# Gate and up products of a column block back to back, and one Block for both halves of the channel mixer

## The chip, the cores and the metric

The kernel runs on one core of a Trainium2 chip. The metric is the device time in microseconds (us) of one execution. Before the change it is 3491.59 us, the median of three runs (3485.54 to 3496.79). A core has five engines, each with its own instruction stream: TensorE (PE in the profile, with its weight loads as PEld), VectorE (DVE), ScalarE (ACT), GpSimd (POOL) and SyncE (SP), which here issues most DMAs. Engines meet only through semaphores.

## The reference, cut to what matters

One decoder layer is computed for 2048 prompt tokens and 8 sample tokens. The change is in its last part, the channel mixer (`conv_ffn`), with the residual sum and the final RMSNorm behind it:

```python
gate, up = jnp.split(h @ w_up, 2, axis=-1)            # D_MODEL 1024 -> 2 x D_FF 2816
g = causal_dwconv(jnp.concatenate([buf, gate], 1), conv_w, conv_b)   # 3 taps along the tokens
f = (jax.nn.silu(g) * up) @ w_down                    # 2816 -> 1024
y = rmsnorm(x2 + f, final_norm_w)
```

The last two gate rows of each group and the sample tokens' gates are outputs too.

## The kernel before, in words

`channel_mixer` (L1848) is called twice by `program`, once for a half of the tokens. Half 1 has 8 tiles of 128 prompt tokens and the 8 sample tokens (9 token tiles, three blocks of 344 columns in a product); half 2 has 8 tiles (two blocks of 512). Each call opens a Block of its own: tensors are placed anew, all engines meet at its end, and nothing of the second call starts before.

Inside, a trip (11 in each half, L1928) works off two column blocks `s` = 0, 1 of D_FF, 128 columns each. Every product is made from a high and a low part of both operands, as three matmuls (hi·hi, hi·lo, lo·hi). In a trip the engines do this, each in the order of its own stream:

- PE: gate products of s=0 into `g_ps`, gate of s=1 into `g_ps`, up of s=0 into `u_ps`, up of s=1 into `u_ps` (`project_up`, L2150 to L2162); then for each token tile n the down product, two 512-column sums of 6 matmuls each (L2182 to L2184), into `y_ps` for even n and into `g_ps` for odd n (`sums`). Tile n waits until the add of tile n-2 has emptied its sum (`added`), and a new trip waits for all adds of the one before (`pe.wait_ge(added, i * YT + 2)`).
- ACT: the high part of the up weights of both s (`up_hi`, L2020), each as soon as PE has done the last product with that buffer; for each s the copies of the gate sums to SBUF (L2026) and the silus (L2030); the high part of both down weights (`dn_hi`, L2035). With the loop closed, `up_hi` of the next trip follows `dn_hi` of this one.
- POOL: `up_lo` = raw - hi of s=0 and of s=1 (L1998, 128x2048), then `dn_lo` of both (L2003, 128x1024), each after its ACT part.
- DVE: `convolve` of s=0 and of s=1 (L2080, L2085), then `multiply` of s=0 and of s=1: for each block gate times up sum (L2113), a CAST to `a_hi` (L2114) and the difference `a_lo` (L2115); then the adds of all token tiles into `y` (L2126). The adds stand behind all of `multiply` in DVE's stream.
- SP: loads, each when its buffer is free.

At a half's start the h tiles are loaded and split into hi and lo (L2011, L2055), and after all of them the first up weights. At its end ACT squares each tile (L2039), one root serves all tiles (L2042), DVE scales them (L2137) and ACT stores them (L2046).

Of the kernel before, what the change touches and what calls it, by code (L numbers as in the profile page):

```python
# [1846 lines left out]
def channel_mixer(nc, tag, sample, first_tile, h2_d, x2_d, w_up_d, w_down_d, small_d, final_w_d,  # L1847
                  edge, y_p_d, y_s_d, s_gate_d):  # L1848
# [4 lines left out]
    TT = TILES // 2  # L1853
    NT = TT * P + (DEC if sample else 0)
    widths = [344] * 3 if sample else [512] * 2
    nb = len(widths)
    at = [sum(widths[:b]) for b in range(nb + 1)]
    assert at[nb] == NT
    YT = TT + (1 if sample else 0)
    NA = YT * P  # L1860
    W = widths[0]
    HALO = FFN_CONV - 1
    TRIPS = FF_TILES // 2
    with ExitStack() as ctx:
# [24 lines left out]
        sq = sb("sq", [P, YT])  # L1889
# [3 lines left out]
        g_ps = ps("g", [P, nb, 512])  # L1893
        u_ps = ps("u", [P, nb, 512])
# [16 lines left out]
        a_hi_ready, a_ready = sem("a_hi_ready"), sem("a_ready")  # L1911
# [15 lines left out]
        def over_trips(eng, body, steps=None, per=0):
            with eng.Fori(0, TRIPS) as i:  # L1928
                if steps:
                    with steps.loop(i, TRIPS, per):  # L1930
                        body(i)
                else:
                    body(i)

        @block.sync
        def _(sp):
            def weights_up(i, s):
                sp.dma_start(up_raw[:, s], w_up_d[bass.ds(i * 2 + s, 1)].rearrange("a p k n -> (a p) k n")
                             ).then_inc(up_landed[s], 16)
# [12 lines left out]
            for n in range(2, len(tiles)):

                sp.wait_ge(h_landed[n % 2], 16 * (n // 2))
                load_h(n)
            for n in range(len(tiles)):
                sp.wait_ge(h_ready, n + 1)
                load_x2(n)

            def body(i):  # L1960
                for s in range(2):

                    sp.wait_ge(conv_ready, (i * 2 + s + 1) * nb)
                    sp.dma_start(small[:, s], small_d[bass.ds(i * 2 + s, 1)].rearrange("a p n -> (a p) n")
                                 ).then_inc(small_landed[s], 16)
                for s in range(2):

                    sp.wait_ge(dn_ready, i * 2 + s + 1)
                    sp.dma_start(dn_raw[:, s], w_down_d[bass.ds((i * 2 + s) * P, P), :]).then_inc(dn_landed[s], 16)

            def ahead(i):
                for s in range(2):

                    sp.wait_ge(up_ready, i * 2 + s + 3)
                    weights_up(i + 1, s)

            with sp.Fori(0, TRIPS - 1) as i:
                body(i)
                ahead(i)
            body(TRIPS - 1)  # L1980

            sp.wait_ge(dn_ready, FF_TILES + 1)
            sp.dma_start(dn_raw[:, 0], final_w_d.rearrange("(a n) -> a n", a=1).broadcast_to([P, D_MODEL])
                         ).then_inc(y_landed, 16)

        @block.gpsimd
        def _(pool):
            pool.memset(a_hi[:, :, NT:].bitcast(F32), 0.0) if sample else None
            pool.memset(a_lo[:, :, NT:].bitcast(F32), 0.0).then_inc(setup, 1) if sample else pool.sem_inc(setup, 1)
# [3 lines left out]
            def body(i):  # L1993
                for s in range(2):

                    pool.wait_ge(up_hi_ready, i * 2 + s + 1)
                    pool.wait_ge(upped, (i * 2 + s + 1) * nb)
                    pool.tensor_tensor(up_lo[:, s], up_raw[:, s], up_hi[:, s].bitcast(F32), ALU.subtract  # L1998
                                       ).then_inc(up_ready, 1)
                for s in range(2):  # L2000
                    pool.wait_ge(dn_hi_ready, i * 2 + s + 1)
                    pool.wait_ge(downed, i * YT + 1)
                    pool.tensor_tensor(dn_lo[:, s], dn_raw[:, s], dn_hi[:, s].bitcast(F32), ALU.subtract  # L2003
                                       ).then_inc(dn_ready, 1)
            over_trips(pool, body)

        @block.scalar
        def _(act):
            for n, (t, c, w) in enumerate(tiles):
                act.wait_ge(h_landed[n % 2], 16 * (n // 2 + 1))  # L2010
                act.activation(h_hi[:, :, c:c + w], stage[:, n, :, 0:w], ACT.Copy).then_inc(h_hi_ready, 1)  # L2011

            act.sem_inc(gate_ready, nb)
            act.sem_inc(act_ready, 1)

            def body(i):
                for s in range(2):
                    act.wait_ge(up_landed[s], i * 16 + 16)
                    act.wait_ge(upped, (i * 2 + s + 1) * nb)
                    act.activation(up_hi[:, s], up_raw[:, s], ACT.Copy).then_inc(up_hi_ready, 1)  # L2020
                for s in range(2):
                    n0 = (i * 2 + s) * nb
                    for b in range(nb):
                        act.wait_ge(gated, n0 + b + 1)
                        act.wait_ge(prod_ready, n0 + nb)
                        act.activation(gate[:, s, HALO + at[b]:HALO + at[b + 1]], g_ps[:, b, 0:widths[b]], ACT.Copy  # L2026
                                       ).then_inc(gate_ready, 1)
                    for b in range(nb):
                        act.wait_ge(conv_ready, n0 + 2 * nb + b + 1)
                        act.activation(gate[:, s, at[b]:at[b + 1]], conv[:, 0:widths[b]], ACT.Silu  # L2030
                                       ).then_inc(act_ready, 1)
                for s in range(2):
                    act.wait_ge(dn_landed[s], i * 16 + 16)
                    act.wait_ge(downed, i * YT + 1)
                    act.activation(dn_hi[:, s], dn_raw[:, s], ACT.Copy).then_inc(dn_hi_ready, 1)  # L2035
            over_trips(act, body)
            for n in range(YT):
                act.wait_ge(added, (TRIPS - 1) * YT + n + 3)
                act.activation(gate[:, 0, 0:D_MODEL], y[:, n], ACT.Square, accum_out=sq[:, n:n + 1]).then_inc(squared, 1)  # L2039
                act.wait_ge(squared, n + 1)  # L2040
            act.wait_ge(mean_ready, 1)
            act.activation(root[:], sq[:], ACT.Sqrt).then_inc(rooted, 1)  # L2042
            for n, (t, c, w) in enumerate(tiles):
                act.wait_ge(y_done, n + 1)
                dst = y_s_d if t == 0 else y_p_d[(t - 1) * P:t * P, :]
                act.dma_start(dst, y[0:w, n]).then_inc(stored, 16)  # L2046
            if sample:
                act.dma_start(s_gate_d, s_gate[:]).then_inc(stored, 16)
            act.wait_ge(stored, 16 * (YT + (1 if sample else 0)))

        @block.vector
        def _(v):
            for n, (t, c, w) in enumerate(tiles):
                v.wait_ge(h_hi_ready, n + 1)
                v.tensor_tensor(h_lo[:, :, c:c + w], stage[:, n, :, 0:w], h_hi[:, :, c:c + w].bitcast(F32),  # L2055
                                ALU.subtract).then_inc(h_ready, 1)
            if sample:
                v.memset(edge[:], 0.0).then_inc(setup, 1)
            else:
                v.sem_inc(setup, 1)  # L2060
            v.wait_ge(setup, 2)
            v.sem_inc(prod_ready, 2 * nb)
            v.sem_inc(conv_ready, 2 * nb)
# [933 lines left out]
```

## Time and profile before

| | us |
|---|---|
| median of the runs | 3491.59 |
| the profiled execution's own time | 3495.07 |
| its span, first to last instruction | 3492.8 |
| PE matmul busy in it | 3033.5 (87%) |
| DVE, ACT, POOL busy | 1599.7, 884.7, 756.5 |

The channel mixer takes the last 1645 us: its first load is issued at 1847.9, half 1's matmuls run from 1880.9 to 2678.2, half 2's from 2728.9 to 3472.3, and the span ends at 3492.8. The granted clock of PE is 1.00 (2.4 GHz) in a steady trip and 0.50 (1.2 GHz) after long pauses. A matmul's record is longer than its step, because matmuls overlap; times of work on PE are best read as the distance from one start to another.

### The profile page before, as it was taken

To read this page: it belongs to the slowest core of one execution; us is meant where nothing else is said; L and a number is where in the kernel's file an instruction comes from. 1 tells how busy PE (TensorE), PEld (TensorE's weight loads), DVE (VectorE), ACT (ScalarE), POOL (GpSimd) and SP (SyncE) were. 2 spreads that over 40 slices of the span, in tenths; PEclk is the share of its full clock that TensorE was granted. 3 is DMA by queue.
4 is the path that set the end of the run, shared out by engine and by line. 5 is a ranking of instruction groups with operands and counts; after the bars stand their busy time and mean duration, and the time that the engine had idled before them with its cause. 6 is when DMAs were issued, how large, how long until landed. Compare 5 with 4: busy or idle time off the path is not lost. (4 is left out here: it accounts for less than half of the span.)

```text
span 3492.8 us, 45919 instructions
## 1 busy us (share of the span) xinstructions
PE 3033.5 (87%) x16539; PEld 2602.2 (75%) x16539; DVE 1599.7 (46%) x2940; ACT 884.7 (25%) x1649; POOL 756.5 (22%) x547
## 2 busy tenths in 40 slices
PE   8999999699997998107894999999996799999997
PEld 6888889576675998006774988998886678878876
DVE  5113111366775888342333544454445434444444
ACT  4123222233332555002223111221112212112212
POOL 4002000244441555002111211122110212211220
PEclk9999999889998999558997999999998899999998
DMA  4454324657752333353435111111102411111101
GB/s 148 177 192 167 112 92 147 166 169 203 201 179 74 85 96 81 105 116 127 144 126 199 48 48 36 36 48 53 44 12 92 157 36 47 60 38 36 60 24 54
DMA packets 227714, 352.66 MB, mean 101 GB/s; under 512 B 73518, under 2 KB 161191, under 8 KB 221592
## 3 DMA queue, kind: packets, MB, share of 16 engines
q1 hardware_dynamic: 219281, 302.07, 28.4%
q10 hardware_dynamic: 7360, 26.34, 1.9%
q0 software_dynamic: 944, 22.61, 1.7%
q8 instruction: 71, 1.16, 0.1%
q14 instruction: 58, 0.48, 0.0%
HBM read 286.16 MB, written 93.95 MB: 109 GB/s over the span
## 5 line engine op out<-in xcount | busy, mean ns | idle before, releaser
L2159 PE MATMUL cm_g_ps<-cm_h_hi,cm_up_hi 128*128 128x344 f32 (+1 forms) x880 | 309.7, 352 | 120.4 <-POOL cm_up_lo L1998 88.3
L2826 PE MATMUL pj_acc<-pj_w_hi,pj_h_hi 128*128 128x480 f32 (+5 forms) x952 | 357.1, 375 | 8.3 <-DVE pj_w_lo L2726 8.3
L2827 PE MATMUL pj_acc<-pj_w_lo,pj_h_hi 128*128 128x480 f32 (+5 forms) x952 | 355.9, 374 | 0.0
L2828 PE MATMUL pj_acc<-pj_w_hi,pj_h_lo 128*128 128x480 f32 (+5 forms) x952 | 355.6, 374 | 0.0
L2003 POOL TENSOR_TENSOR cm_dn_lo<-cm_dn_raw,cm_dn_hi 128x1024 fp32r<-128x1024 f32 x44 | 107.8, 2469 | 995.4 <-ACT cm_dn_hi L2035 995.4
L2161 PE MATMUL cm_g_ps<-cm_h_hi,cm_up_lo 128*128 128x344 f32 (+1 forms) x880 | 307.4, 349 | 0.0
L2160 PE MATMUL cm_g_ps<-cm_h_lo,cm_up_hi 128*128 128x344 f32 (+1 forms) x880 | 307.3, 349 | 0.0
L2159 PE MATMUL cm_u_ps<-cm_h_hi,cm_up_hi 128*128 128x344 f32 (+1 forms) x880 | 306.9, 349 | 0.0
L2161 PE MATMUL cm_u_ps<-cm_h_hi,cm_up_lo 128*128 128x344 f32 (+1 forms) x880 | 305.6, 347 | 0.0
L2160 PE MATMUL cm_u_ps<-cm_h_lo,cm_up_hi 128*128 128x344 f32 (+1 forms) x880 | 305.6, 347 | 0.0
L2159 PEld LDWEIGHTS cm_g_ps<-cm_h_hi,cm_up_hi 128*128 128x128 f32 x880 | 166.6, 189 | 142.8 <-issue 129.2
L1998 POOL TENSOR_TENSOR cm_up_lo<-cm_up_raw,cm_up_hi 128x2048 fp32r<-128x2048 f32 x44 | 204.2, 4642 | 282.9 <-ACT cm_up_hi L2020 282.9
L2026 ACT ACTIVATE cm_gate<-cm_g_ps 128x344 f32<-128x344 f32 (+1 forms) x110 | 55.3, 513 | 799.1 <-PE cm_g_ps L2161 798.2
L2726 DVE TENSOR_TENSOR pj_w_lo<-pj_w_raw,pj_w_hi 128x480 fp32r<-128x480 f32 (+3 forms) x112 | 76.4, 703 | 393.9 <-ACT pj_w_hi L2681 393.9
L2080 DVE TENSOR_SCALAR cm_conv<-cm_gate,cm_small 128x344 f32<-128x344 f32 (+2 forms) x110 | 54.3, 494 | 374.0 <-ACT cm_gate L2030 223.4
L2826 PEld LDWEIGHTS pj_acc<-pj_w_hi,pj_h_hi 128*128 128x128 f32 (+1 forms) x952 | 175.5, 184 | 34.3 <-issue 8.6
L371 POOL TENSOR_TENSOR fp_prod<-fp_kv,fp_q_own 128x1024 f32<-128x1024 f32 x64 | 151.6, 2369 | 226.8 <-DVE fp_s_dec L414 226.8
L2828 PEld LDWEIGHTS pj_acc<-pj_w_hi,pj_h_lo 128*128 128x128 f32 (+1 forms) x952 | 174.9, 184 | 25.9 <-issue 1.3
L2827 PEld LDWEIGHTS pj_acc<-pj_w_lo,pj_h_hi 128*128 128x128 f32 (+1 forms) x952 | 175.0, 184 | 25.1 <-issue 1.0
L2126 DVE TENSOR_TENSOR cm_y<-cm_y,cm_y_ps 128x1024 f32<-128x1024 f32 x99 | 120.9, 1221 | 144.9 <-PE cm_y_ps L2184 144.9
L2659 ACT ACTIVATE pj_row<-pj_acc,pj_rstd 128x480 f32<-128x480 f32 (+6 forms) x119 | 76.2, 641 | 409.0 <-PE pj_acc L2828 373.7
L2159 PEld LDWEIGHTS cm_u_ps<-cm_h_hi,cm_up_hi 128*128 128x128 f32 x880 | 165.2, 188 | 16.0 <-DVE cm_a_lo L2115 2.7
(429 smaller groups left out, 6658.2 us busy)
## 6 DMA issues: line engine op xcount, KB each, us to landing
fp_kv<-in_fox_kv SPq DMA_DIRECT2D x256, 256.0 KB, 3.0
cm_up_raw<-in_w_up SPq DMA_DIRECT2D x44, 1024.0 KB, 4.8
cm_dn_raw<-in_w_down SPq DMA_DIRECT2D x44, 512.0 KB, 3.5
out_s_win<-in_cache POOLq DMA_DIRECT2D x8, 2047.0 KB, 9.6
proj_a<-pj_row SPq DMA_DIRECT2D x48, 240.0 KB
sp_raw<-proj_b SPq DMA_DIRECT2D x16, 640.0 KB, 4.0
pj_w_raw<-in_w_a SPq DMA_DIRECT2D x10, 960.0 KB, 8.1
dp_raw<-proj_a SPq DMA_DIRECT2D x48, 192.0 KB, 3.4
```

The costliest lines, as they stand in the source:

```text
L371: pool.tensor_tensor(prod[:, n % 2], kv[:, at:at + QUART, 0], q_own[:, a // 2:a // 2 + 1].to_broadcast([P, QUART, F]), ALU.mult).then_inc( ...
L1998: pool.tensor_tensor(up_lo[:, s], up_raw[:, s], up_hi[:, s].bitcast(F32), ALU.subtract).then_inc(up_ready, 1)
L2003: pool.tensor_tensor(dn_lo[:, s], dn_raw[:, s], dn_hi[:, s].bitcast(F32), ALU.subtract).then_inc(dn_ready, 1)
L2126: v.tensor_tensor(y[:, n], y[:, n], sums(n).rearrange("p a n -> p (a n)"), ALU.add).then_inc(added, 1)
L2159: pe.matmul(out, hi, h_hi[:, k, cs], start=(k == 0), stop=False)
L2160: pe.matmul(out, hi, h_lo[:, k, cs], start=False, stop=False)
L2161: last = pe.matmul(out, lo, h_hi[:, k, cs], start=False, stop=(k == KT - 1))
L2659: act.activation(row[0:m, n % ROWS, 0:wide], acc[0:m, n % BANKS, 0:wide], ACT.Copy, scale=rstd[0:m, t:t + 1]).then_inc(evac, 1)
L2726: v.tensor_tensor(w_lo[:, j % 2, k, 0:n], w_raw[:, k, 0:n], w_hi[:, j % 2, k, 0:n].bitcast(F32), ALU.subtract).then_inc(w_ready, 1)
L2826: pe.matmul(out, h_hi[:, k, place(t)], w_hi[:, j % 2, k, 0:wide], start=(k == 0), stop=False)
L2827: pe.matmul(out, h_hi[:, k, place(t)], w_lo[:, j % 2, k, 0:wide], start=False, stop=False)
L2828: last = pe.matmul(out, h_lo[:, k, place(t)], w_hi[:, j % 2, k, 0:wide], start=False, stop=(k == KT - 1))
```

## The change

There is one call and one Block; a class `Half` holds the counts of each half, and all tensors keep the sizes of half 1. Four things differ:

1. PE's order in a trip is now gate s=0, up s=0, gate s=1, up s=1, and DVE's is convolve and multiply of s=0, then of s=1. The orders inside ACT's and POOL's trips are the same as before; ACT splits the next trip's up weights at the end of a trip, where it did so at the next one's start.
2. `sums` is counted from the end, so that the last token tile always sums into `y_ps`, and a trip begins when all but the last add are done.
3. The second half's h tiles go through the two `dn_raw` buffers and are split while half 1's last down products run; DVE puts each `finish_h` behind an add. Half 1's squares, root and scaling, and its stores (now on SP, three in flight), run beside half 2's first trip. At the very start the first up weights are split right after the first h tile.
4. The final norm of half 2 is cut into three parts (tiles 0 to 3, 4 and 5, 6 and 7), put between the last adds.

```diff
+        def sums(H, n):
+
+            return y_ps[:] if (H.yt - 1 - n) % 2 == 0 else g_ps[:, 0:2]
...
+            def load_h(m):
...
+                if m in (YT, YT + 1):
+
+                    sp.wait_ge(dn_ready, FF_TILES + m - YT + 1)
+                elif m > YT:
+                    sp.wait_ge(h_ready, m - 1)
+                sp.dma_start(h_raw(m), h2_d[H.tiles[m - H.tile0][0]]).then_inc(h_landed[k], 16)
...
+            split_h(0)
+            split_up(first, 0)
+            for m in range(1, YT):
+                split_h(m)
+            with act.Fori(0, TRIPS - 1) as i:
+                gates(first, i)
+                split_down(first, i)
+                split_up(first, i + 1)
+            gates(first, TRIPS - 1)
+            split_down(first, TRIPS - 1)
+            split_up(second, 0)
+            for m in range(YT, YT + second.yt):
+                split_h(m)
+            squares(first)
...
-            def body(i):
-                convolve(i, 0)
-                convolve(i, 1)
-                multiply(i, 0)
-                multiply(i, 1)
...
+            def middle(H, i):
+                for s in range(2):
+                    convolve(H, i, s)
+                    multiply(H, i, s)
...
+            middle(first, TRIPS - 1)
             for n in range(YT):
...
+                add(first, TRIPS - 1, n)
+                if n > 0:
+                    finish_h(YT + n - 1)
+            v.wait_ge(final_landed, 16)
+            scale_of(first, 0)
+            for n in range(YT):
+                normed(n)
+
+            trip(second, 0)
...
-            def body(i):
-                pe.wait_ge(added, i * YT + 2)
...
+            def trip(H, i):
+                nb, at = H.nb, H.at
+                pe.wait_ge(added, H.down0 + i * H.yt + 1)
                 for s in range(2):
-                    pe.wait_ge(up_ready, i * 2 + s + 3)
-                    project_up(i, s, 0, g_ps, gated)
-                for s in range(2):
-                    project_up(i, s, 1, u_ps, upped)
...
+                    pe.wait_ge(up_ready, H.ff0 + i * 2 + s + 3)
+                    project_up(H, i, s, 0, g_ps, gated)
+                    project_up(H, i, s, 1, u_ps, upped)
...
+                    pe.wait_ge(added, H.down0 + i * H.yt + max(n + 1, 2))
```

PE in half 2's trip, where the gate products of s=0 end (`cm_g_ps` holds gate sums, `cm_u_ps` up sums). Before:

```order
L2159 MATMUL cm_g_ps<-cm_h_hi,cm_up_hi 128x512
L2160 MATMUL cm_g_ps<-cm_h_lo,cm_up_hi 128x512
L2161 MATMUL cm_g_ps<-cm_h_hi,cm_up_lo 128x512
L2167 REGISTER_ALU
L2150 ISA
L2159 MATMUL cm_g_ps<-cm_h_hi,cm_up_hi 128x512
```

And of the change:

```order
L2313 MATMUL cm_g_ps<-cm_h_hi,cm_up_hi 128x512
L2314 MATMUL cm_g_ps<-cm_h_lo,cm_up_hi 128x512
L2315 MATMUL cm_g_ps<-cm_h_hi,cm_up_lo 128x512
L2308 REGISTER_ALU
L2313 MATMUL cm_u_ps<-cm_h_hi,cm_up_hi 128x512
L2314 MATMUL cm_u_ps<-cm_h_lo,cm_up_hi 128x512
```

What came next was the gate of s=1; now it is the up product of s=0, and the gate of s=1 stands a whole product phase later.

DVE in half 2's trip, behind the last `multiply` of s=0. Before:

```order
L2115 TENSOR_TENSOR cm_a_lo<-cm_gate,cm_a_hi 128x512
L2108 REGISTER_ALU
L2113 TENSOR_TENSOR cm_gate<-cm_gate,cm_u_ps 128x512
L75 REGISTER_ALU
L2114 CAST cm_a_hi<-cm_gate 128x512
```

And of the change (the first trip of half 2, which stands unrolled):

```order
L2218 TENSOR_TENSOR cm_a_lo<-cm_gate,cm_a_hi 128x512
L2176 COPY cm_gate<-edge 128x2
L2182 TENSOR_SCALAR cm_conv<-cm_gate,cm_small 128x512
L2187 SCALAR_TENSOR_TENSOR cm_conv<-cm_gate,cm_small,cm_conv 128x512 x2
L2182 TENSOR_SCALAR cm_conv<-cm_gate,cm_small 128x512
```

The convolution of s=1 moved behind the products of s=0; in both, `multiply` of s=1 and then the adds come last.

## Rows read from the trace of the kernel before

**Rows 1.** Waits of the channel mixer: who <- whom, us in total, times, longest.
```profile
PE cm_g_ps L2159 <- POOL cm_up_lo L1998: 88.3, 2, 50.8
PE cm_g_ps L2159 <- DVE cm_y L2126: 32.1, 20, 1.6
```
**Rows 2.** Stretches: length; busy (count) PE, PEld, DVE, ACT, POOL; PEclk, DMA share, GB/s.
```profile
2534.83:2607.30 72.47, 70.86 (x397) 65.59 (x397) 35.77 (x57) 13.67 (x18) 14.24 (x4) 1.00 0.05 15
2534.83:2557.57 22.74, 22.74 (x144) 22.74 (x145) 7.13 (x18) 4.83 (x9) 0.00 (x0) 1.00 0.01 0
...
3136.57:3204.07 67.50, 65.89 (x288) 53.91 (x289) 28.89 (x36) 13.12 (x14) 14.18 (x4) 1.00 0.14 47
3136.57:3158.46 21.89, 21.89 (x97) 18.10 (x97) 6.27 (x11) 4.35 (x6) 0.00 (x0) 1.00 0.00 0
...
3180.33:3202.40 22.07, 22.07 (x97) 17.84 (x95) 10.36 (x10) 1.92 (x1) 4.65 (x1) 1.00 0.14 50
```
**Rows 3.** Order of time, half 2: start, us, engine, instruction, [idle before <-releaser].
```profile
3162.57 1.99 ACT L2035 ACTIVATE cm_dn_hi<-cm_dn_raw 128x1024 fp32r<-128x1024 f32 x2
...
3169.54 1.92 ACT L2020 ACTIVATE cm_up_hi<-cm_up_raw 128x2048 fp32r<-128x2048 f32 x1 [3.67 <-PE cm_u_ps L2161]
...
3163.78 4.93 POOL L2003 TENSOR_TENSOR cm_dn_lo<-cm_dn_raw,cm_dn_hi 128x1024 fp32r<-128x1024 f32 x2 [44.02 <-ACT cm_dn_hi L2035]
...
3182.61 4.65 POOL L1998 TENSOR_TENSOR cm_up_lo<-cm_up_raw,cm_up_hi 128x2048 fp32r<-128x2048 f32 x1 [6.40 <-ACT cm_up_hi L2020]
...
3164.91 1.55 DVE L2114 CAST cm_a_hi<-cm_gate 128x512 fp32r<-128x512 f32 x1
3166.50 2.76 DVE L2115 TENSOR_TENSOR cm_a_lo<-cm_gate,cm_a_hi 128x512 fp32r<-128x512 f32 x1
...
3181.25 0.43 DVE L2114 CAST cm_a_hi<-cm_gate 128x512 fp32r<-128x512 f32 x1
3181.71 0.69 DVE L2115 TENSOR_TENSOR cm_a_lo<-cm_gate,cm_a_hi 128x512 fp32r<-128x512 f32 x1
3183.28 1.22 DVE L2126 TENSOR_TENSOR cm_y<-cm_y,cm_y_ps 128x1024 f32<-128x1024 f32 x1 [0.87 <-PE cm_y_ps L2184]
```
**Rows 4.** The same view, half 1.
```profile
2564.89 4.86 POOL L2003 TENSOR_TENSOR cm_dn_lo<-cm_dn_raw,cm_dn_hi 128x1024 fp32r<-128x1024 f32 x2 [50.21 <-ACT cm_dn_hi L2035]
2571.18 4.75 POOL L1998 TENSOR_TENSOR cm_up_lo<-cm_up_raw,cm_up_hi 128x2048 fp32r<-128x2048 f32 x1 [1.44 <-ACT cm_up_hi L2020]
...
2573.43 2.70 DVE L2114 CAST cm_a_hi<-cm_gate 128x344 fp32r<-128x344 f32 x1
```
**Rows 5.** The same view: PE's first matmuls after three pauses.
```profile
22.08 0.58 PE L2810 MATMUL pj_sum<-pj_ones,pj_sq 128*128 128x1 f32 x2 [5.62 <-POOL pj_sq L2642]
...
321.91 0.58 PE L2810 MATMUL pj_sum<-pj_ones,pj_sq 128*128 128x1 f32 x2 [6.18 <-POOL pj_sq L2642]
...
682.17 1.01 PE L805 MATMUL fp_z<-fp_consts,fp_m_tok 128*4 128x128 f32 x4 [5.89 <-DVE fp_m_tok L626]
```
**Rows 6.** Stretches right after the last two of them, columns as in rows 2.
```profile
321.90:328.10 6.20, 6.19 (x18) 5.82 (x19) 4.90 (x12) 3.21 (x5) 4.21 (x3) 0.50 0.38 120
...
682.20:686.50 4.30, 4.30 (x16) 3.56 (x17) 0.99 (x2) 0.59 (x1) 0.00 (x0) 0.50 0.79 252
```
**Rows 7.** Order of time at the two starts and the end.
```profile
1876.19 9.01 POOL L1998 TENSOR_TENSOR cm_up_lo<-cm_up_raw,cm_up_hi 128x2048 fp32r<-128x2048 f32 x2 [27.77 <-ACT cm_up_hi L2020]
...
2710.28 2.46 DVE L2055 TENSOR_TENSOR cm_h_lo<-cm_y,cm_h_hi 128x1024 fp32r<-128x1024 f32 x2 [5.18 <-ACT cm_h_hi L2011]
...
2720.82 1.23 DVE L2055 TENSOR_TENSOR cm_h_lo<-cm_y,cm_h_hi 128x1024 fp32r<-128x1024 f32 x1 [1.38 <-ACT cm_h_hi L2011]
...
2729.90 0.63 PE L2161 MATMUL cm_g_ps<-cm_h_hi,cm_up_lo 128*128 128x512 f32 x1
2730.33 0.63 PE L2159 MATMUL cm_g_ps<-cm_h_hi,cm_up_hi 128*128 128x512 f32 x1
...
3477.91 9.66 DVE L2137 SCALAR_TENSOR_TENSOR cm_y<-cm_y,cm_rstd,cm_dn_raw 128x1024 f32<-128x1024 f32 x8
```

More of the change, by code:

```diff
@@ L1971, in ahead, with load_small @@
[L1971 to L1975, printed above, removed]
-            with sp.Fori(0, TRIPS - 1) as i:
[L1978 to L1984, printed above, removed]
+            def load_small(H, i, s):
+                if not (H is first and isinstance(i, int) and i == 0):
+                    sp.wait_ge(conv_ready, H.two0 + (i * 2 + s + 1) * H.nb)
+                sp.dma_start(small[:, s], small_d[bass.ds(i * 2 + s, 1)].rearrange("a p n -> (a p) n")
+                             ).then_inc(small_landed[s], 16)
@@ L2041, in _, with squares @@
[L2041 to L2049, printed above, removed]
+            def squares(H):
+                for a, b in norms[halves.index(H)]:
+                    for n in range(a, b):
+                        act.wait_ge(added, H.down0 + (TRIPS - 1) * H.yt + n + 3)
+                        act.wait_ge(squared, H.tile0 + n)
+                        act.activation(gate[:, 0, HALO:HALO + D_MODEL], y[:, n], ACT.Square,
+                                       accum_out=sq[:, halves.index(H), n:n + 1]).then_inc(squared, 1)
+                    if H is second:
+                        act.wait_ge(mean_ready, 2 + norms[1].index((a, b)))
+                    else:
+                        act.wait_ge(mean_ready, 1)
+                    act.activation(root[:, a:b], sq[:, halves.index(H), a:b], ACT.Sqrt).then_inc(rooted, 1)
@@ L2057, in _, with finish_h @@
[L2057 to L2063, printed above, removed]
[L2064 to L2066 removed]
+            def finish_h(m):
+                H = first if m < YT else second
+                _, c, w = H.tiles[m - H.tile0]
+                v.wait_ge(h_hi_ready, m + 1)
+                v.tensor_tensor(h_lo[:, :, c:c + w], h_raw(m)[:, :, 0:w], h_hi[:, :, c:c + w].bitcast(F32),
+                                ALU.subtract).then_inc(h_ready, 1)
@@ new lines, in normed, with trip @@
+            def normed(n):
+                v.scalar_tensor_tensor(out=y[:, n], in0=y[:, n], scalar=rstd[:, n:n + 1], in1=final_w[:],
+                                       op0=ALU.mult, op1=ALU.mult).then_inc(y_done, 1)
+            def trip(H, i):
+                middle(H, i)
+                for n in range(H.yt):
+                    add(H, i, n)
+            for m in range(YT):
+                finish_h(m)
+            v.memset(edge[:], 0.0).then_inc(setup, 1)
+            v.wait_ge(setup, 2)
@@ new lines, in _ @@
+            v.wait_ge(final_landed, 16)
[3 more added lines that the diff above has]
+            trip(second, 0)
+            with v.Fori(0, TRIPS - 2) as i:
+                with dve.loop(i, TRIPS - 2, per[1]):
+                    trip(second, i + 1)
+            middle(second, TRIPS - 1)
+            for n in range(5):
+                add(second, TRIPS - 1, n)
+            scale_of(second, 0)
+            normed(0)
+            add(second, TRIPS - 1, 5)
@@ L2140, in _, with project_up @@
+            normed(1)
+            add(second, TRIPS - 1, 6)
+            normed(2), normed(3)
+            add(second, TRIPS - 1, 7)
+            scale_of(second, 1)
+            normed(4), normed(5)
+            scale_of(second, 2)
+            normed(6), normed(7)
         @block.tensor
         def _(pe):
-            pe.sem_inc(upped, 2 * nb)
+            pe.sem_inc(upped, 2 * NB)
             pe.sem_inc(downed, 1)
-            def project_up(i, s, half, ps_t, done):
+            def project_up(H, i, s, part, ps_t, done):
+                nb, at = H.nb, H.at
@@ L2181, in body @@
                         for k in range(2):
-                            pe.matmul(sums(n)[:, b], a_hi[:, k, ts], dn_hi[:, k, cs], start=(k == 0), stop=False)
-                            pe.matmul(sums(n)[:, b], a_hi[:, k, ts], dn_lo[:, k, cs], start=False, stop=False)
-                            last = pe.matmul(sums(n)[:, b], a_lo[:, k, ts], dn_hi[:, k, cs], start=False,
-                                             stop=(k == 1))
+                            pe.matmul(out[:, b], a_hi[:, k, ts], dn_hi[:, k, cs], start=(k == 0), stop=False)
+                            pe.matmul(out[:, b], a_hi[:, k, ts], dn_lo[:, k, cs], start=False, stop=False)
+                            last = pe.matmul(out[:, b], a_lo[:, k, ts], dn_hi[:, k, cs], start=False, stop=(k == 1))
                     last.then_inc(downed, 1)
-            over_trips(pe, body)
+            for H in halves:
+                with pe.Fori(0, TRIPS) as i:
+                    trip(H, i)
 def dilated_decode(nc, pa, consts_d, rel_d, onehot_d, caches, ma):
```

339 lines of the change are left out of this document (207 added, 132 removed).

## The prediction

> **What bounds the kernel now.** I read the waits first. In the channel mixer PE waits for two things only: twice for the up weights at a half's start (88.3 us, 50.8 of it between the halves), and 20 times, at the start of each trip but a half's first, 1.6 us for the last add [rows 1]. The stretches say the rest: a trip takes 72.47 us in half 1 and 67.50 in half 2 and PE is busy for all of it but that 1.6, at clock 1.00 [rows 2]. So PE bounds it, and DVE, ACT and POOL count only where they make PE wait. That is why the view to look at last, and longest, is the order of time inside one trip: who works beside whom.
>
> There it shows a coupling that costs nothing today. A CAST to a_hi takes 0.43 us and an a_lo 0.69 when POOL is idle; with POOL at dn_lo the same two take 1.55 and 2.76 [rows 3]: the CAST ends 0.2 us after the first dn_lo (3163.78 plus half of 4.93 is 3166.25, the CAST ends at 3166.46), the a_lo 0.55 us after the second (3168.71, 3169.26). In half 1 a CAST beside up_lo takes 2.70 and ends 0.20 after it (2576.13 against 2575.93) [rows 4]. An add (one operand from PSUM) beside up_lo takes its normal 1.22 [rows 3]. So those two DVE instructions wait for the end of the POOL instruction that is under way, whatever its length, and the POOL instruction behind it can get in between them.
>
> **Change 1: the order in a trip.** PE does the same matmuls. I set 0 at the end of the gate products of s=1, today 2557.57 in half 1 and 3158.46 in half 2, the ends of the 22.74 and the 21.89 stretch [rows 2]. Behind that point the chain copy, silu, convolution, dn_hi, dn_lo has the lengths it has now, since it hangs on that point alone today. What moves is how much PE work is left before the down products: both up phases today (21.9 or 22.7 us), one now (half of 21.89 or 22.74: 10.9 or 11.35) [rows 2].
>
> Half 2 [rows 3]: dn_hi runs from 4.1 to 6.1, dn_lo from 5.3 to 10.25. up_hi of s=0 needs only the up products of s=0, long done, so ACT does it at once, by about 9; up_hi of s=1 follows the last up product, 11.1 to 13.1. Hence POOL works without a gap: dn_lo to 10.25, up_lo s=0 to 15.2, up_lo s=1 to 19.9 (4.65 each, and some tenths of waiting for DVE). DVE's products of block 0 start at 5.7 and meet dn_lo as today: a_lo ends at 10.8, PE can start the down products at 11.15 instead of 10.9. Block 1: the product with the up sum (0.7, like an a_lo) 11.2 to 11.9, then the CAST waits for up_lo s=0, to 15.4, and a_lo for up_lo s=1, to 20.5. The adds stand behind it in DVE's stream: the first ends at 21.7, and PE goes on at 22.1 (DVE to PE takes 0.3 today). PE has done token tiles 0 and 1 by 11.15 + 5.5 = 16.65 (22.07 us for eight, 2.76 each [rows 2]), and tile 2 needs the first add. Stall 5.45, with the late start 5.7. The alternating sums take the 1.6 away. A trip: 67.5 - 1.6 + 5.7 = 71.6.
>
> Half 1 [rows 4]: dn_lo runs from 7.3 to 12.2, so the down products start at 12.45, 1.1 late. The a_lo of block 1 ends at 12.6; in block 2 the CAST waits for up_lo s=0 (to 17.0) and a_lo for up_lo s=1 (to 21.7), ending at 22.1; the first add ends at 23.3, PE goes on at 23.6, where it was due at 12.45 + 5.6 = 18.05. Stall 5.55. A trip: 72.5 - 1.6 + 1.1 + 5.55 = 77.5.
>
> In all: half 1 has 11 such trips and 1.8 of slow start, 854.3 against 797.3 today (1880.9 to 2678.2): +57. Half 2 has nine of 71.6, a last one without weights to split (66.1), and a first one in which DVE comes late from half 1's norm, which I put at 72.5 (bounds 67 and 78): 783 against 743.4: +40.
>
> No row shows an a_lo held by an up_lo that follows at once on the one that held its CAST; dn_lo does exactly that in every trip [rows 3]. The bounds for this wait are 0.7 (it slips in before) and 4.7 + 0.7; I take the upper one, since the pair of dn_lo is the nearest row.
>
> The Trainium skill, SBUF: State Buffer, section "SBUF: two separate sides", has the rule: VectorE and GpSimd share a port pair, an exclusive lock that whoever starts first holds for its whole instruction, and an instruction of VectorE with two SBUF inputs needs it too. By it the sum is the one above. The same page names the other reading, shared bandwidth, and rejects it; by that one the a_lo would be stretched to about 2.8 as in rows 3, and the sum would be near that of the first rival. The ends of CAST and a_lo just behind the ends of POOL's instructions speak for the lock.
>
> **What the stall does to PE's clock.** After pauses of 5.62, 6.18 and 5.89 us [rows 5] the granted clock was 0.50, for the next 6.2 us after the second and 4.3 after the third [rows 6]; across each 1.6 it stayed 1.00 [rows 2]. At 0.50 a 512-column matmul steps 0.43 (2729.90 to 2730.33 [rows 7]) against 0.23, so a mean of 5.3 us loses 5.3 x 0.46 = 2.4. With 20 stalls of 5.5 us the bounds are 0 and 60; I take 45, nine in ten of them.
>
> The Trainium skill, TensorE: Matmul & The Clock Gate, section "What's actually happening", advises to put the cost of ramping up below 1% of a typical kernel. By it these 45 would be under 35 us. The rows speak against it here, since the pause comes back in every trip.
>
> **Change 2: alternating sums.** Worth the 32.1 us [rows 1], already in the trips. Cover: the add of the last tile but one (1.22) lies beside the last tile's 2.76.
>
> **Change 3: one Block.** The up weights of half 2 are split in half 1's last trip, and the h tiles one behind each add. Today the last six h_lo take from 2710.28 to 2722.05 [rows 7], 2.0 us a tile; two tiles in flight instead of a queue of loads make it some 2.7, beside 2.8 (more at the slow clock) of down products a tile: the eighth ready near 48 on the clock of that trip, PE at half 2's second block near 51. So the 50.7 between the halves goes: -51 (bounds -51 and -35). ACT's nine squares and DVE's nine scalings (9.66 for eight [rows 7]) are moved beside half 2's first trip, PE's first two phases cover most of them; SP's stores stand ahead of that trip's x2 loads and of the second trip's small and down weights, all landed by about 45 to 60, when the first add is due at 53. At the very start POOL's first up_lo, at 1876.19 [rows 7], moves to about 1856 and its second to 1861.5; the first products then wait for h tile 2, whose h_lo waits for that second up_lo, to 1868.7 instead of 1880.9: -12 (bounds -14 and -6).
>
> **Change 4 and the rest.** The cut norm saves about 5 of the last tail (four scalings before and two behind the last root instead of eight [rows 7]), but its first part stands ahead of add 5 on DVE, 4.4 us long, where PE has 1.5 to spare before add 5 and one more tile: +4. Together -1 (bounds -5 and +4). Down products take 25.4 us for nine tiles in half 1, 2.82 each, and 2.76 in half 2; the tensors are placed anew, and nothing in PE's work differs. I take -5 for the pair (bounds -7 and +7, the difference on 9 or 8 tiles in 11 trips, either way).
>
> Sum: +57 + 40 + 45 - 51 - 12 - 1 - 5 = +73. The profiled execution took 3495.07 (span 3492.8), 3.5 over the median; the sum on the median: 3491.6 + 73 = 3565.
>
> **Rivals.**
> - a_lo slips in between the two up_lo. Place: DVE behind the last CAST of a trip. Half 1: a_lo ends at 17.7, add at 18.9, PE goes on at 19.2, stall 1.15; half 2: 16.1, 17.3, 17.6, stall 0.95. That is 11 x 4.4 + 9 x 4.5 = 89 less, and pauses of 1 us leave the clock alone, 45 less: 3431. It decides in the 0.04 us between CAST and a_lo. For it: up_lo s=1 must be ready on POOL in time (it is by 2 us); against it: the second dn_lo gets in, in every trip.
> - The stalls come, the clock stays: 3520. The pauses are a little shorter than the shortest of the three rows; but no longer one kept the clock.
> - The change does what it seems to: DVE never meets POOL. 32 + 51 + 12 + 1 + 5 less, about 3391. Against it: POOL's 14 us of work must lie between dn_hi and the next trip, and DVE's last block lies at its start.
> - The h chain between the halves is 2 us a tile slower than I have it and holds PE at half 2's second block: 13 more, 3578.
>
> **How the numbers follow.** Forecast 0.66; a_lo slips in 0.12; clock stays 0.12; no meeting 0.04; h chain 0.06. The time is 3565. The range 3500 to 3592 takes in the clock that stays and the upper bounds of the first trip, the norm and the clock; both cases on the fast side lie below it. 0.3% is 10.5 us, about what a measurement of this kernel can tell from no change: faster 0.16, the two fast cases; same 0.04, the lower edge of the clock case; slower 0.80.
>
> **What would show it.** In the new trace: PE waits for DVE's add at the third token tile, 20 times, 5 to 6 us; last-block CAST and a_lo of 3.5 to 5 us in most trips; PEclk below 1.00 in every trip; trips of 79 to 80 and 73 to 74 us; no gap between the halves; PE's first product near 1869. Wrong I am if last-block a_lo is 0.7 in all trips, or if PE's pauses are under 2 us.

## The result, and the profile after

The changed kernel took 3552.34 us (median of 4 runs, 3543.50 to 3558.39), the kernel before 3490.64 (4 runs, 3485.54 to 3496.79): a ratio of 1.0174, 95% interval 1.0146 to 1.0202, so 61.7 us slower. Forecast were 3565 in a range of 3500 to 3592, and slower with 0.80. The profiled execution of the new kernel took 3543.50 (span 3541.4), at its lower end.

First the waits of the channel mixer (columns as in rows 1), answering to [rows 1].

```profile
PE cm_y_ps L2337 <- DVE cm_y L2231: 53.9, 11, 4.9
PE cm_g_ps L2337 <- DVE cm_y L2231: 43.7, 9, 4.9
PE cm_y_ps L2337 <- POOL cm_dn_lo L2077: 9.2, 9, 1.1
PE cm_g_ps L2313 <- DVEq L2257: 30.9, 1, 30.9
```

The last of these is the start, PE's wait for its first product. The 20 short waits for an add at a trip's start are gone, and so is the second wait for up weights. In their place stand 20 waits of 4.9 us for an add ahead of a down product, 97.6 us in all. In the text that follows, a pause is such a wait.

Now the stretches, cut at the same five marks: from the last h tile of the stage before (L1780) to PE's first product, half 1, the gap between the halves, half 2, and the end. Of before:

```profile
1843.42:1880.94 37.52, 0.00 (x1) 0.03 (x1) 11.31 (x11) 13.70 (x12) 5.29 (x4) 0.50 0.83 308
1880.94:2678.35 797.41, 781.13 (x4356) 723.11 (x4356) 390.97 (x627) 154.51 (x211) 151.44 (x43) 1.00 0.13 42
2678.35:2729.07 50.72, 0.16 (x1) 0.19 (x2) 22.80 (x24) 16.09 (x15) 4.90 (x2) 0.55 0.77 292
2729.07:3472.48 743.41, 727.36 (x3168) 594.72 (x3168) 318.70 (x395) 147.20 (x165) 150.88 (x43) 1.00 0.13 45
3472.48:3492.80 20.32, 0.00 (x0) 0.00 (x0) 11.93 (x15) 2.64 (x4) 0.00 (x0) 0.57 0.51 208
```

Of after, where the gap has no length; behind them a trip of half 1, its first two token tiles with the pause, the 4.9 us that follow the pause, and a trip of half 2:

```profile
1829.68:1860.54 30.86, 0.00 (x1) 0.03 (x1) 14.41 (x12) 11.98 (x11) 9.57 (x4) 0.50 0.80 291
1860.54:2724.94 864.40, 799.13 (x4357) 739.29 (x4357) 458.48 (x632) 156.36 (x203) 156.98 (x44) 0.96 0.15 49
2724.94:3525.66 800.72, 754.03 (x3169) 608.49 (x3167) 397.11 (x422) 157.67 (x185) 151.35 (x42) 0.97 0.15 53
3525.66:3541.40 15.74, 0.00 (x0) 0.00 (x0) 9.54 (x19) 2.60 (x6) 0.00 (x0) 0.66 0.53 213
...
2332.41:2410.90 78.49, 72.56 (x398) 67.11 (x396) 41.12 (x57) 13.78 (x18) 14.26 (x4) 0.96 0.12 40
2378.90:2389.53 10.63, 5.71 (x25) 4.43 (x25) 10.56 (x6) 0.94 (x1) 9.07 (x2) 0.90 0.52 161
2389.53:2394.44 4.91, 4.91 (x12) 3.90 (x13) 1.07 (x1) 0.00 (x0) 0.00 (x0) 0.52 0.49 197
...
3016.62:3090.58 73.96, 69.11 (x290) 55.76 (x288) 35.59 (x36) 13.01 (x14) 14.66 (x4) 0.95 0.13 43
```

The stages up to the first mark are the same code in both kernels, and yet the mark lies at 1843.42 in one execution and 1829.68 in the other. In the twelve traces of this document it lies between 1829.7 and 1844.8, about as far apart as the runs of one kernel lie, so stretches behind the mark are the better comparison. Behind it the kernel before takes 1649.38 us and the changed one 1711.72, a difference of +62.3, near the 61.7 between the medians. It is +67.0 in half 1, +57.3 in half 2, -50.7 between them, -6.7 at the start and -4.6 at the end. The nine trips of half 2 between its first and last take 73.6 us on the average.

One trip of half 2 in the order of time (columns as in rows 3; gate products of s=1 end at 3050.09):

```profile
3055.35 4.96 POOL L2077 TENSOR_TENSOR cm_dn_lo<-cm_dn_raw,cm_dn_hi 128x1024 fp32r<-128x1024 f32 x2 [58.29 <-ACT cm_dn_hi L2119]
3060.28 5.08 POOL L2072 TENSOR_TENSOR cm_up_lo<-cm_up_raw,cm_up_hi 128x2048 fp32r<-128x2048 f32 x1
3065.31 4.70 POOL L2072 TENSOR_TENSOR cm_up_lo<-cm_up_raw,cm_up_hi 128x2048 fp32r<-128x2048 f32 x1
...
3056.60 1.45 DVE L2217 CAST cm_a_hi<-cm_gate 128x512 fp32r<-128x512 f32 x1
3058.08 2.77 DVE L2218 TENSOR_TENSOR cm_a_lo<-cm_gate,cm_a_hi 128x512 fp32r<-128x512 f32 x1
3061.45 0.69 DVE L2216 TENSOR_TENSOR cm_gate<-cm_gate,cm_u_ps 128x512 f32<-128x512 f32 x1 [0.59 <-PE cm_u_ps L2315]
3062.18 3.45 DVE L2217 CAST cm_a_hi<-cm_gate 128x512 fp32r<-128x512 f32 x1
3065.66 4.89 DVE L2218 TENSOR_TENSOR cm_a_lo<-cm_gate,cm_a_hi 128x512 fp32r<-128x512 f32 x1
3070.48 1.21 DVE L2231 TENSOR_TENSOR cm_y<-cm_y,cm_g_ps 128x1024 f32<-128x1024 f32 x1
...
3071.74 0.80 PE L2337 MATMUL cm_g_ps<-cm_dn_hi,cm_a_hi 128*128 128x512 f32 x1 [4.85 <-DVE cm_y L2231]
```

Against [rows 3], POOL's four subtractions now form one block from 3055.35 to 3070.01. The last block's CAST ends at 3065.63, 0.3 us after the first up_lo (3065.35), and its a_lo at 3070.55, 0.5 after the second. So the CAST, which had been waiting, got in when the first up_lo ended; the a_lo came 0.03 us behind it and found the second up_lo under way. The add stands behind them in VectorE's stream, and PE waits for the add. The product with the up sum (3061.45) began beside the same up_lo and took its usual 0.69.

### The profile page after: what moved, and what is told of

Its sections match the earlier page's. It is cut to its first block and busy times, and to the rows that moved or that the text cites. A ratio compares the mean times of both kernels' runs of the same rounds, so it can differ in the third digit from the quotient of the medians.

```text
span 3541.4 us, 45796 instructions
## 1 busy us (share of the span) xinstructions
PE 3064.3 (87%) x16539; PEld 2621.2 (74%) x16539; DVE 1722.9 (49%) x2952; ACT 879.2 (25%) x1647; POOL 761.2 (21%) x547
## 5 line engine op out<-in xcount | busy, mean ns | idle before, releaser
L2313 PE MATMUL cm_g_ps<-cm_h_hi,cm_up_hi 128*128 128x344 f32 (+1 forms) x880 | 309.0, 351 | 30.9 <-DVEq L2257 30.9
L2337 PE MATMUL cm_y_ps<-cm_dn_hi,cm_a_hi 128*128 128x512 f32 x396 | 167.4, 423 | 65.3 <-DVE cm_y L2231 53.9
L2218 DVE TENSOR_TENSOR cm_a_lo<-cm_gate,cm_a_hi 128x344 fp32r<-128x344 f32 (+1 forms) x110 | 196.4, 1785 | 3.8
L2337 PE MATMUL cm_g_ps<-cm_dn_hi,cm_a_hi 128*128 128x512 f32 x352 | 146.9, 417 | 46.0 <-DVE cm_y L2231 43.7
```

The source lines that it names most:

```text
L2218: v.tensor_tensor(a_lo[:, s, cs], g, a_hi[:, s, cs].bitcast(F32), ALU.subtract).then_inc(prod_ready, 1)
L2313: pe.matmul(out, hi, h_hi[:, k, cs], start=(k == 0), stop=False)
L2337: pe.matmul(out[:, b], a_hi[:, k, ts], dn_hi[:, k, cs], start=(k == 0), stop=False)
```

## The experiments

Each was measured beside the kernel before on the same chip, so a difference is taken to that neighbour (3488.15 for e1 to e4, 3488.71 for e5 to e8, 3493.55 for e9 and e10); the changed kernel's own was 61.7 over its neighbour.

**e1: the order of a trip put back, everything else kept.**

```diff
 for s in range(2):
     pe.wait_ge(up_ready, H.ff0 + i * 2 + s + 3)
     project_up(H, i, s, 0, g_ps, gated)
+for s in range(2):
     project_up(H, i, s, 1, u_ps, upped)
...
-for s in range(2):
-    convolve(H, i, s)
-    multiply(H, i, s)
+convolve(H, i, 0)
+convolve(H, i, 1)
+multiply(H, i, 0)
+multiply(H, i, 1)
```

> One Block and alternating sums, but in a trip PE and VectorE go in the order of before: gate products of both column blocks, then up products of both. Theory (the whole loss is the new order: POOL's up_lo runs beside VectorE's last products, the first add comes late, PE stalls and its clock falls): no stall at token tile 2, granted clock 1.00 in all trips, a trip of about 70.1 us in half 1 (72.47 less the 1.6 wait, less 0.75 for the shorter down step) and 66.8 in half 2 (67.5 less 1.6, plus 1.0 for the longer gate and up step); time 3491 less 95 = about 3396. Rival (the one Block or the other parity of the sums costs something of its own, a stall at another add): over 3440.

Measured: 3400.59 (3397.23 to 3406.78) against 3488.15, ratio 0.9753 [0.9737, 0.9769]. Its trips, one of each half (columns as in rows 2):

```profile
2575.42:2645.25 69.83, 69.83 (x398) 65.59 (x396) 42.56 (x63) 18.11 (x23) 14.11 (x4) 1.00 0.19 54
3052.20:3118.62 66.42, 66.42 (x289) 54.07 (x288) 28.71 (x36) 13.12 (x14) 14.19 (x4) 1.00 0.14 48
```

In these trips PE is busy throughout at clock 1.00. So one Block and the sums gain 87.6 us, and the order costs 149.3 (61.7 lost and 87.6 not gained). One pause was left that nobody had expected, in half 2's first trip:

```profile
2662.64 0.80 PE L2314 MATMUL cm_g_ps<-cm_h_hi,cm_up_hi 128*128 128x512 f32 x1 [6.08 <-ACT cm_gate L2108]
```

ScalarE's nine squares of half 1's norm, 1.24 us each, stand ahead of its gate copies there. With the clock that gate phase takes 30.7 instead of 22.3 us.

**e2: new order kept, both of POOL's up_lo behind VectorE's products.**

```diff
 pool.wait_ge(upped, H.two0 + (i * 2 + s + 1) * H.nb)
+pool.wait_ge(prod_ready, H.two0 + i * 2 * H.nb + 2 * H.nb)
```

> The changed kernel, its new order kept, but POOL's two up_lo of a trip wait until VectorE has finished the products of the trip before. Theory (VectorE's last CAST and a_lo wait for the ends of the two up_lo, and that alone stalls PE and lowers its clock): both take 0.4 and 0.7 us again, no stall at token tile 2, clock 1.00, trips of about 71.2 and 66.9 us (one wait of 1.0 for dn_lo is left in half 1); time about 3407. Rival (the first add is late because the order leaves VectorE too little time, whatever POOL does): pauses of 3 us and more remain and the time stays above 3500. Rival 2 (POOL now is late for the next trip's up weights): PE waits at a trip's start instead.

Measured: 3415.48 (3412.45 to 3421.36), ratio 0.9800 [0.9783, 0.9816]. A trip of each half:

```profile
2443.98:2515.10 71.12, 70.11 (x397) 65.57 (x396) 33.23 (x57) 13.78 (x18) 14.03 (x4) 1.00 0.14 45
2863.73:2930.15 66.42, 66.42 (x290) 54.07 (x288) 28.54 (x36) 13.01 (x14) 14.13 (x4) 1.00 0.15 48
```

The last block's two instructions, which took 3.45 and 4.89, here:

```profile
2909.27 0.43 DVE L2218 CAST cm_a_hi<-cm_gate 128x512 fp32r<-128x512 f32 x1
2909.73 0.69 DVE L2219 TENSOR_TENSOR cm_a_lo<-cm_gate,cm_a_hi 128x512 fp32r<-128x512 f32 x1
```

PE, ScalarE and VectorE execute the same instructions in the same order as in the changed kernel; only when POOL subtracts is different. That returns 134.4 us of the 149.3. The wait for dn_lo is left (1.3 us a trip in half 1 against e1), and with it the new order is still 14.9 us slower than the old one (3415.48 against 3400.59, side by side): even mended, it gains nothing here. In no trip does PE wait for late up weights; once, in half 1's last, it waited 1.7 for an add. VectorE has time enough in this order.

**e3: only the second up_lo behind the products.** The same line, for s == 1 alone.

> The changed kernel, but only POOL's second up_lo of a trip waits for VectorE's products of the trip before; the first runs where it ran. This makes the case that the forecast took as its first rival. Theory (an instruction of VectorE waits for the end of POOL's instruction that is under way, then goes): the last CAST still takes about 3.5 to 4.2 us, a_lo 0.7, PE's pause at token tile 2 is 0.9 to 1.2 us instead of 4.9, the clock stays at 1.00; time 3552 less 20 x 3.8 less 48 for the clock = about 3428. If POOL and VectorE merely shared a bandwidth: CAST and a_lo would each change in proportion to the overlap, with ends that do not coincide with POOL's.

Measured: 3427.30 (3423.55 to 3430.53), ratio 0.9828 [0.9812, 0.9845], 1 us from the number expected. The order of time in half 2:

```profile
2914.75 5.08 POOL L2074 TENSOR_TENSOR cm_up_lo<-cm_up_raw,cm_up_hi 128x2048 fp32r<-128x2048 f32 x1
2920.91 4.60 POOL L2074 TENSOR_TENSOR cm_up_lo<-cm_up_raw,cm_up_hi 128x2048 fp32r<-128x2048 f32 x1 [1.09 <-DVE cm_a_lo L2220]
...
2916.65 3.45 DVE L2219 CAST cm_a_hi<-cm_gate 128x512 fp32r<-128x512 f32 x1
2920.14 0.69 DVE L2220 TENSOR_TENSOR cm_a_lo<-cm_gate,cm_a_hi 128x512 fp32r<-128x512 f32 x1
...
2922.02 0.50 PE L2339 MATMUL cm_g_ps<-cm_dn_hi,cm_a_hi 128*128 128x512 f32 x1 [0.65 <-DVE cm_y L2233]
```

The CAST beside an up_lo takes the same 3.45 as before and ends as that up_lo ends (2920.10 against 2919.83); the a_lo with no up_lo queued takes 0.69. With the second up_lo queued it took 4.89. So an instruction of VectorE waits for the whole instruction of POOL that is under way, and gets in when that one ends; the next of VectorE's finds POOL's next one running, if that stood ready.

**e4: the late add kept, PE kept busy meanwhile.** The 20 extra products are read by nobody.

```diff
+if n == 2:
+    for _ in range(20):
+        pe.matmul(g_ps[:, 2], a_hi[:, 0, 0:P], dn_hi[:, 0, 0:512], start=True, stop=True)
 pe.wait_ge(added, H.down0 + i * H.yt + max(n + 1, 2))
```

> The changed kernel, but ahead of its wait at token tile 2 PE does 20 matmuls of 512 columns whose result nobody reads (20 x 0.227 = 4.5 us). The late add stays as late, so only the clock is changed. Theory (the stall costs 4.9 us directly and some 2.3 more through the lower clock behind it): granted clock 1.00 in the trips, 20 x 2.4 = 48 us less, plus 9 us in the two trips that have no stall: about 3513. Rival (the low clock costs nothing, because the late weights and adds set the end of a trip anyway): 3552 to 3561.

Measured: 3518.87 (3512.62 to 3525.36), ratio 1.0093 [1.0074, 1.0111]. A trip of each half:

```profile
2401.79:2478.19 76.40, 74.93 (x417) 69.27 (x416) 41.19 (x57) 13.77 (x18) 14.34 (x4) 1.00 0.13 41
2927.04:2998.69 71.65, 71.25 (x310) 57.79 (x308) 35.67 (x36) 13.01 (x14) 14.73 (x4) 1.00 0.14 44
```

Clock 1.00, and a trip is 2.0 us shorter in the mean of each half, though PE does 20 products more and goes on at the same add. PE still waits 0.4 to 0.5 us behind the 4.54 of extra products, so filling and wait together are 0.1 longer than the pause was. The clock thus costs 2.1 us in each of the 20 trips, about 42 in all. The kernel as a whole gains less, 31 us, because the two trips without a pause do the 20 products for nothing (4.6 and 4.8 us longer).

**e5 and e6: the order alone, and the sums alone, in the kernel before.**

```diff
 # e5, PE; on VectorE convolve and multiply of one s follow one another too
     project_up(i, s, 0, g_ps, gated)
-for s in range(2):
     project_up(i, s, 1, u_ps, upped)
...
 # e6
-return y_ps[:] if n % 2 == 0 else g_ps[:, 0:2]
+return y_ps[:] if (YT - 1 - n) % 2 == 0 else g_ps[:, 0:2]
-pe.wait_ge(added, i * YT + 2)
+pe.wait_ge(added, i * YT + 1)
-pe.wait_ge(added, i * YT + n + 1)
+pe.wait_ge(added, i * YT + max(n + 1, 2))
```

> The kernel before, with the new order of a trip alone (PE: gate and up products of one column block, then of the other; VectorE: convolution and products of one, then of the other); two Blocks, sums as before. Theory: in all trips but a half's last (no up weights follow there) VectorE's last CAST and a_lo wait for POOL's up_lo, PE stalls 4.9 us at token tile 2 and loses 2.3 (half 1) or 1.9 us (half 2) more through its clock; half 1 waits 1.0 for dn_lo in 11 trips; the 1.6 at a trip's start stays. 20 x 4.9 + 10 x 2.3 + 10 x 1.9 + 11 = +151, about 3639. Rival (the stall comes from the up weights of the next half or the sums' parity, not from the order): under 3550.

> The kernel before with the alternating sums alone (a half's last token tile always in y_ps, so the next trip's gate products needn't wait for its add). Theory: the 20 waits of 1.6 us at a trip's start go and nothing takes their place: 3488 less 32 = 3456. Rival (an add becomes late elsewhere, since the first tile of half 2 now uses g_ps, which the gate copies must have left): 3470 to 3490.

Measured: e5 3649.24 (3642.15 to 3654.41), ratio 1.0456 [1.0433, 1.0480]; e6 3450.73 (3447.93 to 3458.23), ratio 0.9895 [0.9873, 0.9916]. PE's waits in e5, and one trip of each half of e6:

```profile
PE cm_y_ps L2180 <- DVE cm_y L2125: 97.5, 20, 5.0
PE cm_g_ps L2158 <- DVE cm_y L2125: 32.2, 20, 1.7
PE cm_y_ps L2180 <- POOL cm_dn_lo L2003: 9.1, 9, 1.0
```

```profile
2581.99:2652.61 70.62, 70.62 (x397) 65.49 (x395) 33.41 (x57) 17.76 (x31) 4.85 (x2) 1.00 0.02 7
2771.79:2837.40 65.61, 65.61 (x290) 53.99 (x288) 28.90 (x36) 13.12 (x14) 14.18 (x4) 1.00 0.15 48
```

The order alone makes the 20 pauses, without one Block and without the sums, and costs 160.5 us. The sums gain 38.0, not 32: a trip shrinks by 1.85 and 1.89 us ([rows 2]: 72.47 and 67.50) where the profile shows a wait of 1.6. A wait is counted from the modelled end of the last matmul, which lies 0.16 after the start that the next one would have had, and behind the wait the first step is 0.31 and not 0.23 (3136.57 to 3136.88 in the kernel before).

**e7: other addresses, no instruction changed.**

```diff
-h_hi = sb("h_hi", [P, KT, NT], F32R)         # h_lo as well
+h_hi = sb("h_hi", [P, KT, NT + 8], F32R)
...
+shift = sb("shift", [P, 8])
 a_hi = sb("a_hi", [P, 2, NA], F32R)
```

> The changed kernel with its tensors placed otherwise and no instruction changed: rows of h_hi and h_lo are 4160 bytes apart instead of 4128, and 8 floats in front move a_hi and a_lo from a byte address of 0 to one of 32 (mod 64), where they were in half 1 of the kernel before. Theory (the step of a matmul depends on where its operands begin): gate and up products of half 2 step 227.0 ns as in half 2 of before instead of 232.4; down products step 234.2 instead of 227.2 in both halves; of the time -11.4 and up to +16, less what the stall at token tile 2 hides. Rival (the steps differ for another reason, as what the other engines write meanwhile): both steps stay at 232.4 and 227.2.

Measured: 3559.94 (3554.54 to 3565.35, 2 runs), ratio 1.0203 [1.0174, 1.0231]. Mean steps from one matmul's start to the next: down products 233.2 and 233.3 ns in the two halves against 227.2 in the changed kernel; gate and up products of half 2 231.7 against 232.4. The first half of the theory held: with a_hi and a_lo 32 bytes off, every down product takes 6 ns more than 227. (The longer rows move both tensors by another 512 bytes; e8 has that move alone and keeps 226.9.) The second failed: rows 4160 bytes apart took no more than 0.7 ns off. The traces hold no addresses; those given here follow from the sizes of the tensors ahead in the kernel.

**e8: e1 with two more edits: the rows of e7's first edit, and VectorE's releases of the first trip ahead of its nine h_lo.**

```diff
-for m in range(YT):
-    finish_h(m)
 v.memset(edge[:], 0.0).then_inc(setup, 1)
 v.wait_ge(setup, 2)
 v.sem_inc(prod_ready, 2 * NB)
 v.sem_inc(conv_ready, 2 * NB)
 v.sem_inc(added, 2)
+for m in range(YT):
+    finish_h(m)
```

> One Block and alternating sums with the old order of a trip (as e1), and two things more: h_hi and h_lo rows 4160 bytes apart, and VectorE's increments that release PE's first trip ahead of its nine h_lo instead of behind them. Theory: gate and up steps of half 2 fall from 232.4 to 227.0 ns (192 x 11 x 5.4 = 11.4 us); PE's first product begins some 8 us earlier, when three h_lo are done and not nine: 3400.6 less 11 less 8 = about 3381. Rival (the start is bound by the h tiles of the later column blocks, so PE only begins earlier and waits then; placement is without effect): 3400.

Measured: 3390.35 (3385.42 to 3391.78), ratio 0.9713 [0.9695, 0.9731]. From the first mark to PE's first product it is 24.4 us, 6.4 less than the 30.9 of e1 and of the changed kernel. The step of half 2's gate and up products stayed at 231.7, so of the 19 us that were expected against e1 10.8 came.

**e9: as e8, but half 2's rows of h_hi and h_lo 4096 bytes apart.**

```diff
+def rows_of(t, H):
+    return t[:, 0:KT * H.nt].rearrange("p (k n) -> p k n", k=KT)
...
+h_hi, h_lo = rows_of(h_hi_t, H), rows_of(h_lo_t, H)
```

> As e8, but with h_hi and h_lo at their old addresses and only half 2's rows in them 4096 bytes apart, as in half 2 of the kernel before (half 1's stay at 4128). Theory (the moving rows' distance sets the step): gate and up products of half 2 step 227.0 ns instead of 232; 192 x 11 x 4.7 = 10 us less than e8's 3390, about 3380. Rival (other addresses, as those of the up weights or the instruction stream, set it): 232 ns and 3391.

Measured: 3375.11 (3369.55 to 3385.74) against 3493.55, ratio 0.9669 [0.9645, 0.9693]. Gate products of a trip in half 2, 96 matmuls, e8 and then e9:

```profile
2710.37:2732.62 22.25, 22.25 (x97) 18.03 (x96) 7.56 (x13) 5.63 (x7) 0.00 (x0) 1.00 0.00 0
```

```profile
2701.32:2723.08 21.76, 21.76 (x97) 18.02 (x96) 7.56 (x13) 5.63 (x7) 0.00 (x0) 1.00 0.00 0
```

The engines do the same beside them, and the step is 226.7 against 231.8 ns in these stretches. Tensors behind h_hi lie up to 512 bytes elsewhere in e8; in e1 all begin where they do in e9 and only half 2's rows lie otherwise, 4128 bytes apart, and there the gate products step 232.3. This is the fastest version here, 118 us under its neighbour.

**e10: as e9, half 2's first two gate copies ahead of the nine squares on ScalarE.** The squares' scratch output goes to the other half of `gate`, since the copies now fill the first.

> As e9, and ScalarE copies half 2's first two gate blocks ahead of the nine squares of half 1's norm instead of behind them. Theory: PE's one pause of 5.9 us in half 2's first trip goes, and the low clock behind it (6.8 us at half speed, some 3): about 9 us less than e9, near 3371. Rival (VectorE's nine scalings of that norm then hold the first trip's products, and PE waits at its down products instead): as e9.

Measured: 3382.49 (3382.05 to 3387.60), ratio 0.9688 [0.9672, 0.9704], not faster than e9. The pause moved:

```profile
2676.17 0.80 PE L2330 MATMUL cm_u_ps<-cm_h_hi,cm_up_hi 128*128 128x512 f32 x1 [16.54 <-DVE cm_a_lo L2233]
```

The rival was right, one place earlier than it said. VectorE waits for that norm's root, does its nine scalings and only then half 2's first convolution, so PE's second up phase waits 16.5 us for products. The norm itself has to move, not the copies.

## Why the prediction was nearly right

**The likeliest case was the one that came.** The place (token tile 2, 20 times), the holder (POOL's two up_lo), and the way through VectorE's last CAST and a_lo were forecast and are shown by e2: with POOL alone moved, the pauses are gone and 134.4 us return. The first rival, worth 0.12, was made real by e3 and gave 3427, where the prediction had 3431. What separates it from the forecast is whether the second up_lo is ready when the first ends. The rival of a slower h chain (0.06) fell too: half 2's first trip shows no wait for an h tile.

The Trainium skill, SBUF: State Buffer, section "SBUF: two separate sides", gave the rule of an exclusive lock held for a whole instruction, and rejected the reading of a shared bandwidth. The runs agree with the rule: 3.45 beside one up_lo in the changed kernel and in e3 alike, both with the end 0.3 us behind the up_lo's, then 4.89 with another queued and 0.69 without.

**The sum, +73 forecast and +62.3 measured, by stretches** (with the clock, the term for the steps and the +4 for a pause before add 5 put to the halves): half 1 +79 and +67.0; half 2 +62 and +57.3; between the halves -51 and -50.7; start -12 and -6.7; the tail behind PE's last product -5 and -4.6. That half 2 came so close is luck in part: its steps were 12 us worse than forecast, and pauses, sums and the +4 some 14 better.

- *The stalls* were taken as 5.45 to 5.7 and are 4.85 to 4.92. VectorE's instructions ended where the prediction had them (the a_lo 20.5 us after the gate products; that the prediction halved merged rows of POOL did no harm: taken singly, the first dn_lo of [rows 3] ends at 3166.18 and the CAST 0.3 behind it), but PE went on within 0.1 us of the add's end, not 0.3 to 0.4, and began to wait 0.1 later. With dn_lo's wait and the clock a trip's loss from the order is 8.7 in half 1 (78.49 less e1's 69.83) where 8.9 was forecast, and 7.2 in half 2 (73.6 less 66.4) where 7.95 was: some 9 us less in all.
- *The clock* was 45 and is 42 by e4. The rival that it stays, 0.12, fell: the clock was down at all 20 pauses. The Trainium skill, TensorE: Matmul & The Clock Gate, section "What's actually happening", advises to put ramping up below 1% of a typical kernel. Measured are 42 of 3552 us, 1.2%, because the pause comes back in nearly every trip.
- *The sums* gain 38.0 and not 32.1 (e6).
- *The term for the down products' steps*, "nothing in PE's work differs", -5, is the step that failed in kind. Two effects of where operands lie hide in it. In half 1 a_hi and a_lo moved from 32 to 0 (mod 64 bytes): 234.2 to 227.2 ns, 108 x 11 x 7.0 = 8.3 us gained. In half 2 the rows of h_hi and h_lo went from 4096 to 4128 bytes apart: 227.0 to 232.4 ns, 192 x 11 x 5.4 = 11.4 lost; half 2's down step gave 1.8 back. Together +1. The bound of +7 held it, but the two products of half 2 that pay it weren't even looked at. e7 shows the first effect, and e9 against e1 the second.
- *The start* was half as good. PE was to go at the third h_lo; but VectorE's increments of prod_ready, conv_ready and added stand behind all nine, and PE's wait names that queue (L2257 above). e8 moves them and gets 6.4 us.
- *The end*: the tail was right (-5 and -4.6). The +4 for the norm's first part ahead of add 5 didn't show; PE has no pause in half 2's last trip.

**One Block** did what was said: no gap. Its own cost appears where the old order takes the stalls away: the 6.08 us of e1 behind half 1's squares. The changed kernel hides it, since PE needs the second gate phase later.

What stays open: the expected +151 for e5 was 160.5. Its trace puts the 10 us into half 2, where a trip grows by 7.7 us (75.16 less 67.50) and 6.8 was expected: the pauses are 5.0 us and the clock stays low for 4.9 to 6.0 behind each, where the changed kernel's half 2 has 4.85, and 2.9 to 6.2 behind them. Why its pauses are longer isn't shown. Which address rule lies behind 227 and 232 ns wasn't found, only that 4096 bytes give the one and 4128 and 4160 the other.

## What to carry to other kernels

When an order of products is changed, list what the other engines do in the stretch that becomes shorter. In this kernel a CAST or subtraction of VectorE with all operands in SBUF that met a subtraction of GpSimd waited for its whole rest, and the next one for a second if two were queued. When such a pair stands on the path to PE, one wait on the engine that isn't on the path (e2) mends it: it turned 61.7 us lost into 72.7 gained. But compare with leaving the order alone too: that gained 87.6 (e1). A pause of 5 us in a loop is worth avoiding, or filling (e4), because PE paid for it again through its clock.

## What the runs showed of the hardware

- A CAST and a two-operand subtraction in SBUF on VectorE (0.43 and 0.69 us) take 3.45 and 4.89 us when two GpSimd subtractions of 4.6 to 5.1 us stand back to back. In the changed kernel 42 CASTs, 20 a_lo of 512 columns and one h_lo began beside a subtraction of GpSimd that ran on past their usual end, and all ended behind it. With an operand in PSUM none was held: 42 products with an up sum kept 0.50 to 0.52 (344 columns) and 0.69 (512), and an add beside up_lo its 1.22 (e2).
- In 20 of 20 pauses of 4.85 to 4.92 us PE's granted clock fell to 0.50 (1.2 GHz), for 2.9 to 6.2 us behind the pause, at a mean price of 2.1 us. A pause of 2.3 us in half 2's first trip lowered it in the changed kernel, e4 and e7 and left it at 1.00 in e2 and e3; after pauses of 0.3 to 1.7 us it stayed 1.00.
- A 512-column fp32r matmul steps 227 ns with its stationary operand at an address of 0 mod 64 bytes and 233 to 234 at 32 (addresses worked out from the tensors' sizes); with moving rows 4096 bytes apart it steps 227, with 4128 or 4160 apart 232.
